# Sample-token projection moved out of the k loop and into four column groups (hybrid decoder step, one core)

## What is computed

```python
q, k, v, qi, ki, wi = jnp.split(x @ w_in, A_SPLIT_POINTS, axis=-1)
ki = layer_norm(ki, idx_g, idx_b)
# later, for each query: score = sum over heads of relu(qi . ki) * wi ; top-k of it
```

## Time and profile before

| quantity | value |
| --- | --- |
| median of 3 runs | 1205.24 us (1202.90 to 1206.31) |
| profiled execution, its own time | 1206.22 us |
| its span, first to last record | 1204.5 us |
| PE busy | 1161.0 us (96%) |
| DVE, ACT busy | 891.1 us (74%), 558.5 us (46%) |
| mean granted clock of PE | 0.991 |
| chain that ended last | PE 79%, DVE 14%, ACT 2% |

### The profile page before, as it was taken

The page is one execution under the profiler, slowest core; times in us unless marked ns, Lnnn a source line. Parts: engine busy times, 40 slices in busy tenths (PEclk is TensorE's granted clock), DMA queues, the critical chain, the costliest instruction groups (busy, mean ns, idle before and its releaser), DMA issues.

```text
span 1204.5 us, 24770 instructions
## 1 busy us (share of the span) xinstructions
PE 1161.0 (96%) x9290; PEld 1067.3 (89%) x9294; DVE 891.1 (74%) x1759; ACT 558.5 (46%) x1012; POOL 91.6 (8%) x141
## 2 busy tenths in 40 slices
PE   8999988999999999999999999899999999999995
PEld 3959844589999999999999988699999999999995
DVE  2279999857899488586777667778896795795676
ACT  2342158744654353443334566645642443543334
POOL 4424400200000000000500000000000000000000
PEclk9999989999999999999999999899999999999998
DMA  7676580143223324233433211042223233233322
GB/s 213 176 223 221 154 261 15 45 136 105 70 70 115 94 75 138 70 106 106 157 104 107 73 57 53 12 149 70 71 71 123 87 106 92 85 106 105 90 86 71
DMA packets 62704, 128.45 MB, mean 107 GB/s; under 512 B 8027, under 2 KB 36859, under 8 KB 62475
## 3 DMA queue, kind: packets, MB, share of 16 engines
q1 hardware_dynamic: 52699, 114.38, 30.2%
q0 software_dynamic: 3360, 6.56, 1.8%
q10 hardware_dynamic: 6544, 6.17, 1.6%
HBM read 122.52 MB, written 5.86 MB: 107 GB/s over the span
## 4 chain that ended last, share of the span: by engine, by line
PE 79%; DVE 14%; ACT 2%; issue 2%; DMA 1%; SPq 1%; ACTq 0%; DVEq 0%
PE PS L718 34%; PE PS L915 20%; PE PS L750 12%; PE PS L1233 3%; PE PS L1045 2%; PE PS L1001 2%; PE PS L986 2%; PE PS L1015 1%; DVE SC L2480 1%; DVE MX L2478 1%; DVE PB L2306 1%; DMA KVR<-cacheV 1%; DVE MSK L2489 1%; SPq L479 1%; PE PS L1179 1%
## 5 line engine op out<-in xcount | busy, mean ns | idle before, releaser
L718 PE MATMUL PS<-XH,WHI 128*128 128x260 f32 x1088 | 221.8, 285 | 0.7 <-DVE XL L2349 0.7
L718 PE MATMUL PS<-XH,WLO 128*128 128x260 f32 x1088 | 219.4, 283 | 0.0
L718 PE MATMUL PS<-XL,WHI 128*128 128x260 f32 x1088 | 219.1, 283 | 0.0
L718 PEld LDWEIGHTS PS<-XH,WHI 128*128 128x128 f32 x1088 | 167.6, 189 | 5.9 <-issue 4.8
L718 PEld LDWEIGHTS PS<-XH,WLO 128*128 128x128 f32 x1088 | 167.8, 189 | 0.0
L718 PEld LDWEIGHTS PS<-XL,WHI 128*128 128x128 f32 x1088 | 167.4, 188 | 0.0
L1295 ACT ACTIVATE WHI<-WRAW 128x1024 fp32r<-128x1024 f32 x72 | 76.3, 1059 | 178.4 <-PE PS L718 136.3
L1826 DVE TENSOR_TENSOR WLO<-WRAW,WHI 128x1024 fp32r<-128x1024 f32 x64 | 79.3, 1238 | 98.8 <-ACT WHI L1295 98.7
L915 PE MATMUL PS<-HH,RNH 128*128 128x260 f32 x384 | 109.2, 284 | 2.4 <-DVE RNL L1966 2.4
L915 PE MATMUL PS<-HL,RNH 128*128 128x260 f32 x384 | 108.5, 283 | 0.0
L915 PE MATMUL PS<-HH,RNL 128*128 128x260 f32 x384 | 108.5, 283 | 0.0
(11 more groups left out here) (349 smaller groups left out, 2797.7 us busy)
## 6 DMA issues: line engine op xcount, KB each, us to landing
WRAW<-wall SPq DMA_DIRECT2D x168, 512.0 KB, 3.7
BT<-bias_skewed SPq DMA_DIRECT2D x16, 256.0 KB, 5.0
X<-xT SPq DMA_DIRECT2D x4, 520.0 KB, 6.9
X<-xT SPq DMA_DIRECT2D x1, 2080.0 KB, 11.3
yT<-X SPq DMA_DIRECT2D x8, 260.0 KB
KVB<-cacheK SPq DMA_DIRECT2D x16, 128.0 KB, 3.3
KVX<-cacheK SPq DMA_DIRECT2D x16, 128.0 KB, 3.2
KVB<-cacheK POOLq DMA_DIRECT2D x16, 128.0 KB, 3.9
```

The source lines that it names most:

```text
L718: mm = pe.matmul(PS[:, 2 * slot + g, 0:TG], tile, x[:, k, TG * g:TG * g + TG], start=(k == 0 and w is w_hi and x is hi), stop=(k == KT - 1 ...
```

## The change

The sample tokens leave the k loop. After it, eight matmuls take the last 32 tokens of x (24 prompt tokens and the 8 samples) as weights, k tile k in column group k mod 4: PSUM partitions 32 (k mod 4) to 32 (k mod 4) + 31 of bank 4, two k tiles summing up in each group. ACT copies bank 4, now four partial sums, to a new tile NPART. In unit 0, ahead of its third k tile, one matmul with a new 0/1 constant (C_NEW) adds the four partial sums and takes out the 8 sample rows, into bank 5; ACT copies them to NAT. Unit 0 waits for four NAT copies instead of five; the fifth is waited for ahead of unit 2's transposes. The constants grow by 8 columns.

```diff
--- before.py
+++ after.py
@@ -203,7 +203,7 @@
 
 
 
-C_ID, C_ONE, C_CAUS, C_WIN, C_WD, C_BLK, C_SAM, C_END = 0, 128, 256, 384, 640, 704, 832, 840
+C_ID, C_ONE, C_CAUS, C_WIN, C_WD, C_BLK, C_SAM, C_NEW, C_END = 0, 128, 256, 384, 640, 704, 832, 840, 848
 H_SEQ, H_DEC, H_WIN, H_END = 0, 640, 640 + 1025, 640 + 1025 + 128
 
 
@@ -218,6 +218,7 @@
     for b in range(DB):
         c[b, C_WD + 8 * b:C_WD + 8 * b + 8] = 1.0
         c[NH * b:NH * b + NH, C_SAM + b] = 1.0
+        c[32 - DB + b::32, C_NEW + b] = 1.0
         c[NH * b + 1:NH * b + NH, C_BLK + NH * b:C_BLK + NH * b + NH] = 1.0
     h = np.concatenate([one_hot(511 - np.arange(640)), one_hot(PAST - np.arange(PAST + 1)),
                         one_hot(P - 1 - np.arange(P))], axis=1)
@@ -291,6 +292,7 @@
         MK0 = place("MK0", [P, P], BF16, at=hw + 7472)
         DG = place("DG", [P, P], at=hw + 7344)
         PD = place("PD", [P, 1025], at=hw + 4096)
+        NPART = place("NPART", [P, NATW], at=hw + 7864)
         KW = BT[:, 0:DB, 0:129]
         PBB = place("PBB", [P, 2, 1024], at=0)
         words[0] = xw + 16640 + NH * 512
@@ -414,6 +416,7 @@
         hh_done, hl_done = sem("hh_done"), sem("hl_done")
         x_hi, x_lo = sem("x_hi"), sem("x_lo")
         nat_mm, nat_ev = sem("nat_mm"), sem("nat_ev")
+        np_ev, np_sum = sem("np_ev"), sem("np_sum")
         kstat, ksd, kid = sem("kstat"), sem("ksd"), sem("kid")
         kit_mm, kit_ev = sem("kit_mm"), sem("kit_ev")
         seq_mm, seq_ev = sem("seq_mm"), sem("seq_ev")
@@ -1040,18 +1043,28 @@
             for k in range(KT):
                 if k % 2 == 0:
                     pe.wait_ge(x_in[k // 2], 32)
-                for t in range(5):
-                    m = P if t < QT else DB
-                    mm = pe.matmul(PS[0:m, t, 0:NATW], X32[:, k, t * P:t * P + m], WN[:, k, :],
+                for t in range(QT):
+                    mm = pe.matmul(PS[:, t, 0:NATW], X32[:, k, t * P:t * P + P], WN[:, k, :],
                                    start=(k == 0), stop=(k == KT - 1))
                     if k == KT - 1:
                         mm.then_inc(nat_mm, 1)
+            for k in range(KT):
+                r = slice(32 * (k % 4), 32 * (k % 4) + 32)
+                mm = pe.matmul(PS[r, 4, 0:NATW], X32[:, k, TOK - 32:TOK], WN[:, k, :],
+                               start=(k < 4), stop=(k >= 4))
+            mm.then_inc(nat_mm, 1)
+
+            def sample_tokens():
+
+                pe.wait_ge(np_ev, 1)
+                pe.matmul(PS[0:DB, 5, 0:NATW], CST[:, C_NEW:C_NEW + DB], NPART[:],
+                          start=True, stop=True).then_inc(np_sum, 1)
 
             pe.wait_ge(cst_in, 16 * 10)
             pe.matmul(PS[0:16, 6, 0:512], TAB[:], CHS[:, 0:512], start=True, stop=True)
             pe.matmul(PS[0:16, 7, 0:P], TAB[:], CHS[:, 512:640], start=True, stop=True
                       ).then_inc(seq_mm, 1)
-            pe.wait_ge(nat_ev, 5)
+            pe.wait_ge(nat_ev, 4)
             pe.wait_ge(x_lo, 1)
             items = [(t, h) for t in range(1, QT) for h in range(IDXH)]
             spans = ((0, 512), (512, 1024), (1024, 1025))
@@ -1097,6 +1110,7 @@
             for u in range(STATIC_UNITS):
                 if u == 2:
 
+                    pe.wait_ge(nat_ev, 5)
                     pe.wait_ge(kid, 1)
                     for t in range(QT):
                         pe.transpose(PS[:, 4, t * P:(t + 1) * P],
@@ -1121,6 +1135,8 @@
                                for k in range(KT)}
                 elif u == 6:
                     between = {2: sample_sums}
+                elif u == 0:
+                    between = {2: sample_tokens}
                 else:
                     between = {0: lambda: digit(slot), 4: lambda: digit(slot + 1)}
                 unit(u, u % 2, XH, XL, between)
@@ -1653,11 +1669,14 @@
             high_part(0, 0)
             high_part(1, 1)
             act.wait_ge(z_nat, 1)
-            for t in range(5):
-                m = P if t < QT else DB
+            for t in range(QT):
                 act.wait_ge(nat_mm, t + 1)
-                nc.scalar.activation(NAT[0:m, t, :], PS[0:m, t, 0:NATW], ACT.Copy
-                                     ).then_inc(nat_ev, 1)
+                nc.scalar.activation(NAT[:, t, :], PS[:, t, 0:NATW], ACT.Copy).then_inc(nat_ev, 1)
+            act.wait_ge(nat_mm, 5)
+            nc.scalar.activation(NPART[:], PS[:, 4, 0:NATW], ACT.Copy).then_inc(np_ev, 1)
+            act.wait_ge(np_sum, 1)
+            nc.scalar.activation(NAT[0:DB, 4, :], PS[0:DB, 5, 0:NATW], ACT.Copy
+                                 ).then_inc(nat_ev, 1)
             act.wait_ge(seq_mm, 1)
             nc.scalar.activation(SEQS[:], PSF[0:16, 3072:3072 + 640], ACT.Copy
                                  ).then_inc(seq_ev, 1)
```

## The result

The changed kernel's median is **1207.59 us** (20 runs, 1203.50 to 1213.06), that of the kernel before, run beside it, 1205.39 us (20 runs, 1202.85 to 1206.84). The ratio of the times is 1.0025, with an interval of 1.0015 to 1.0036: slower by about 2.2 us where a gain of 0.9 was forecast, and above the range's upper end of 1206.1. The profiled execution took 1211.37 us with a span of 1209.7, which is 5.15 us more than before (1206.22) and 3.8 us more than its own kernel's median. So its trace shows the loss at more than its median size.

The account below looks back on a forecast made before the run. PE (TensorE) was taken to bound the kernel. Of a 3.9 us head start 0.9 us was to survive: 1206.22 - 0.9 = 1205.3 us, less 1.0 for the median, 1204.3 us; range 1202.0 to 1206.1.

Parts of the forecast that it names:

- What bounds: Whole kernel: PE, busy 96% of the span; everything behind 75.9 us is released by DVE or PE progress.
- the terms up to unit 2: Projection to unit 2: removed matmuls -6.0 us, packed ones +1.3, matmul inside unit 0 0.77; transposes 3.9 us early.
- The doubt about a change of form inside unit 0: Unit 0: changing the tiling mode drains the engine, against the matmul placed there; 0.77 us against 0.57.
- The lead that reaches unit 5: PE at units 2 to 4: readiness of WLO lets unit 4 be early by 2.4 us at the most.
- The landing of unit 6's weights: Sync queue and ACT: issued at 59.25, landed 4.0 us later at 63.25; split at 64.19 can be 0.9 us early.
- The step that failed: Unit 5: PE, 2.4 us ahead, waits for RS copies queued behind ACT's split; 0.9 us of gain remains.
- C: PE idling before units 2, 3 and inside unit 5 lowers the clock, costing 3.3 us: 1207.6 us; chance 0.05.
- A: Unit 6's weights land over 1.5 us sooner, unit 4's 2.4 us becomes the limit: 1202.8 us; chance 0.10.
- B: Projection: column groups don't overlap, ACT's new wait delays the sync queue: 1205.5 to 1206.0 us; chance 0.07.
- D: V-page transfers, which hold PE to 163.24 us, absorb the 0.9 us: 1205.2 us; chance 0.13.
- The forecast's own conditions: Wrong if sync queue issues move, unit 6's weights land outside 63 to 63.6, or 0.9 us is missing at 163 us.

Follow-up runs that it names:

- the loop alone: Kernel before with the eight sample matmuls moved behind the k loop, one column group, no packing, no partial sums: 1204.43 us, 0.9994.
- the one with the delay: Kernel before with five useless ACT copies of 128x512 ahead of the split of unit 6's weights: 1212.25 us, 1.0050.

## Why the prediction was wrong

**What bounds, and the terms up to unit 2: right.** Packed eight 1.31 us (predicted 1.3), unit 0 at 28.8 (29.5: PE's first matmul starts 0.2 us earlier, and the loop freed 0.4 us more than the 6.0 counted), partial sums' matmul 0.72 (0.77), SEQS copied by 32.2 (33.1) before the queue needs it, transposes at 41.26 (41.9), all issues of weights in place, a wait on WLO of 0.89 us ahead of unit 2, unit 6's split released by the transfer. The doubt about a change of form inside unit 0 changed nothing.

**The lead that reaches unit 5: too small.** "Unit 4 can be early by 2.4 us at the most" was read from one trace in which unit 4's WLO was ready at 55.63. In the trace after it was ready at 54.65, and PE came to unit 5 with 3.33 us of lead (60.67 for 64.00). The stop there had to take up 3.3 us and not 2.4.

**The landing of unit 6's weights: mis-sized.** I took 4.0 us from one transfer of one trace and got 0.9 us of lead out of it. It took 5.09 in the trace after. Across the traces of the changed kernel the split started at 63.09, 64.04 and 64.36, with 62.65 in the loop alone. Both parts of it vary: the queue issued the transfer at 58.62, 59.59, 59.19 and 58.38, and the split followed the issue by 4.47, 4.45, 5.17 and 4.27 us. The forecast gain was within the scatter of the date it rested on, and each microsecond that the split is late goes straight into PE's wait.

**The step that failed** is "PE, having 2.4 us of lead, waits inside unit 5 for the RS copies (four banks in rotation) and loses the rest there". I counted that as free: a lead that is lost costs nothing. It took 2.90, 1.9 and 1.9 us in three traces, and in each PE's granted clock was 0.50 for 13.7 us of full work behind it. That cost 6.0 to 6.2 us, the largest term of the whole account, and it had no place in my sum. In the traces where the wait was filled, shorter, or without its cause the clock stayed at 1.00; making the wait in the kernel before brought the half clock.

**The rivals.** C was the right one, at 0.05. That its time, 1207.6 us, is the measured median to the digit is luck: the three traces with the half clock took over 1211 us, and the median mixes such executions with others. I named the place among others and then argued it away with "the new waits are a microsecond or less each", though the step above had already put 1.5 us, the lead of 2.4 less the 0.9 that was to arrive, into that single wait; with weights that land no earlier than before it is all 2.4. I also sized it at 3.3 us, from the 6.6 us of half clock in the earlier trace rows; here it lasted 13.7. The Trainium skill, "TensorE: Matmul & The Clock Gate", Part 1, says that an idle TensorE loses its clock, and the prediction set its rule aside because no row showed how short an idle time does it; the trace agrees in kind, with 2.90 us idle and 0.51 behind it. A, B and D did not happen: the lead did not pass on, the column groups do overlap, and what DVE lost did reach the end.

The forecast's own conditions held in part: the queue's issues stood, the split was released as said; it was wrong by "if unit 6's weights land elsewhere than 63 to 63.6", and even a split at 63.09, which one of the three traces had, ended in the half clock.

**What stays open.** Which executions of the changed kernel fall to half clock, and on what that hangs: a wait of 1.9 us was followed by it in two traces, waits of 1.23 and 0.81 were not in one trace each, but these kernels had different work ahead of the wait. Why the queue's issue varies by 1.2 us and the transfer by 0.9. Why 4 of the 126 runs of the kernel before, at 1211.86 to 1213.74 us with a mean clock of 0.984 to 0.987, look like slow runs of the changed one; none of them has a trace here. And where part of the head start goes further down: with the split moved, DVE's gap is 3.6 us early and the median 1.9; that trace has a new wait in the attention stage (PE's waits, 140 to 185 us),

```profile
PE PS L1004 <- DVE PB L2363: 4.4, 3, 3.4
```

of 4.4 us in three pieces, the longest 3.4, which in the kernel before was 0.6. The second trace of that kernel has 1.3 us there, the longest 0.7, and its median gained more; but one trace of each does not show that this wait is the difference.

## What to carry to other kernels

When a head start must be lost before the next fixed date, ask where the engine will stand and for how long, not only how much is lost: one wait of 2 to 3 us ahead of a stretch in which TensorE sets the pace cost more here, in each trace that has it, than the whole head start was worth. Look then at the order of the engine that is waited for: moving one weight split behind eight short copies on ScalarE turned 1.0025, 1.0036 and 1.0010 of the time before into 0.9985 and 0.9965. And a gain that rests on one transfer's landing needs that landing from more than one execution, and so does a lead that one trace is said to allow.

## What the runs showed of the hardware

The half clock outlasts its cause by far. Read in stretches of half a microsecond, it holds for 13.7 us in each of the three traces of the changed kernel (66.2 to 79.9, 65.8 to 79.5 and 64.7 to 78.3) and for 10.2 us in the one with the delay (67.7 to 77.9). PE is busy all through once the wait is over, and the clock goes back to full in the middle of a unit with no change in the work. I had expected full work to bring it back sooner, by the 6.6 us of the earlier trace rows. Nor does it begin with the first matmul behind the wait: in the trace with the delay it fell 0.7 us before that matmul, with PE idle. The first line is of that trace, the second of the changed kernel's, where the half clock ends:

```profile
67.50:68.00 0.50, 0.00 (x0) 0.00 (x0) 0.00 (x0) 0.50 (x3) 0.17 (x1) 0.66 0.72 170
```

```profile
79.50:80.00 0.50, 0.50 (x2) 0.01 (x1) 0.00 (x0) 0.50 (x2) 0.00 (x0) 0.59 0.95 338
```

Half the clock did not double the time of this mix: 8.8 us of matmuls took 14.8 to 15.0, of which 13.7 were at half clock. At exactly half speed those 13.7 would have cost 6.8 us; they cost 6.0 to 6.2.

Four column groups of fp32 matmuls cost no more than one also at 328 columns: 16 records in 1.31 us, which with 0.44 for the last leaves 0.29 us from one round of four records to the next, the price of a single full record in the earlier trace rows. An estimate by the 2.38 times for three column tiles that was set against it (the Trainium skill, "TensorE: Matmul & The Clock Gate", Part 3) was 1.9 us; the trace sides with the earlier trace rows.

An 8-column fp32 matmul costs as much as a full-width one: eight in a row took 4.58 us, 0.57 each, as a 128-column one does. The 0.77 us of the earlier trace rows is the price of standing alone between full ones.
